# The last twelve expert rows in smaller batches, and the first mixer tile requested at another point, in a two-block float32 kernel

## What is computed

```
def one_block(args):
    xb, ib, gb = args
    ue = jnp.take(u, ib, axis=0)
    a = jnp.einsum('thkd,td->thk', ue, xb, preferred_element_type=jnp.float32)
    w = jax.nn.gelu(a) * gb
    ve = jnp.take(v, ib, axis=0)
    return jnp.einsum('thk,thkd->td', w.astype(ve.dtype), ve)
```

## Time and profile before

| what | value |
|---|---|
| runs | 1396.99, 1397.28, 1399.54 us (median 1397.28) |
| the profiled execution | 1396.25 us, its span 1394.4 us |
| mean granted TensorE clock | 0.962 of full speed |
| PE busy | 1263.6 us |
| DVE busy | 726.9 us |
| gathers | 256, from 297.0 to 954.6 us (issue times) |
| DMA rate while gathers run | about 420 GB/s |

### The profile page before, as it was taken

How to read it: one execution, slowest core, us unless ns; L and a number is a source line. 1 busy time by engine, 2 the same in 40 slices (tenths; PEclk the granted TensorE clock), 3 DMA queues, 4 the chain that set the end, 5 groups by cost and what they waited for, 6 DMA issues and landing times.

```text
span 1394.4 us, 12560 instructions
## 1 busy us (share of the span) xinstructions
PE 1263.6 (91%) x4528; PEld 723.0 (52%) x4528; DVE 726.9 (52%) x1760; ACT 239.9 (17%) x614; POOL 321.8 (23%) x273
## 2 busy tenths in 40 slices
PE   7999999989989888778889897878999999999998
PEld 6757555465545444333334332333456458888743
DVE  3664623178767777777786875654244532100001
ACT  2132221111211111111221112111201431000000
POOL 0100000024434444353545545452000010000000
PEclk9999999999999999898999999999999999999999
DMA  8435577269999999999999999997335363543530
GB/s 292 173 130 181 181 253 275 86 266 422 388 418 421 421 418 420 415 421 407 414 422 421 421 407 421 421 420 320 136 128 181 129 249 133 182 168 111 191 150 31
DMA packets 98669, 398.97 MB, mean 286 GB/s; under 512 B 6384, under 2 KB 9840, under 8 KB 65712
## 3 DMA queue, kind: packets, MB, share of 16 engines
q0 software_dynamic: 37376, 270.29, 46.8%
q1 hardware_dynamic: 61232, 127.88, 25.7%
HBM read 397.09 MB, written 1.05 MB: 286 GB/s over the span
## 4 chain that ended last, share of the span: by engine, by line
PE 61%; DMA 21%; DVE 13%; issue 2%; ACT 2%; POOL 1%; SPq 0%; DVEq 0%; PEldq 0%; ACTq 0%
DMA big<-in_peer_uv,idx_t 21%; PE ps L500 15%; PE ps L512 14%; PE ps L750 10%; DVE big L1795 6%; PE ps L1024 5%; PE ps L719 2%; PE ps L689 2%; PE ps L988 2%; PE ps L972 2%; PE ps L526 1%; POOL big L1396 1%; PE ps L592 1%; ACT rows L1211 1%; PE ps L489 1%
## 5 line engine op out<-in xcount | busy, mean ns | idle before, releaser
L750 PE MATMUL ps<-big,rows 128*128 128x512 f32 x1024 | 491.2, 636 | 103.2 <-ACT rows L1211 103.2
L1396 POOL DMA_INDIRECT big<-in_peer_uv,idx_t x256 | 309.1, 1207 | 391.6 <-PE ps L750 328.8
L750 PEld LDWEIGHTS ps<-big,rows 128*128 128x128 f32 x1024 | 203.2, 203 | 373.2 <-issue 373.2
L1795 DVE CUSTOM_DVE_ANT_0 big<-big 128x1024 f32<-128x1024 f32 x256 | 307.7, 1224 | 144.9 <-DMA big<-in_peer_uv,idx_t 142.1
L500 PE MATMUL ps<-wring,big 128*128 128x512 f32 (+1 forms) x496 | 211.6, 582 | 0.0
L512 PE MATMUL ps<-big,wring 128*128 128x256 f32 x896 | 195.6, 381 | 1.0 <-DVE big L1450 1.0
L512 PEld LDWEIGHTS ps<-big,wring 128*128 128x128 f32 x896 | 171.2, 191 | 25.2 <-issue 1.8
L500 PEld LDWEIGHTS ps<-wring,big 128*128 128x128 f32 x496 | 93.4, 191 | 107.7 <-issue 106.5
L1205 ACT ACTIVATE small<-small 128x4 f32<-128x4 f32 x64 | 13.2, 207 | 513.5 <-DVE small L1800 513.5
L1211 ACT ACTIVATE rows<-const,small 128x128 f32<-128x128 f32 x256 | 81.9, 391 | 19.2 <-DVE small L1804 18.0
L1024 PE MATMUL ps<-wring,big 128*128 128x512 f32 x176 | 75.7, 592 | 0.0
(11 more groups left out here) (243 smaller groups left out, 944.0 us busy)
## 6 DMA issues: line engine op xcount, KB each, us to landing
wring<-in_w_in SPq DMA_DIRECT2D x17, 2048.0 KB, 8.2
wring<-in_w_ada SPq DMA_DIRECT2D x12, 2048.0 KB, 8.6
wring<-in_w_gate SPq DMA_DIRECT2D x5, 2048.0 KB, 7.7
wring<-in_w_up SPq DMA_DIRECT2D x5, 2048.0 KB, 7.9
wring<-in_w_down SPq DMA_DIRECT2D x5, 2048.0 KB, 8.4
wring<-in_w_out SPq DMA_DIRECT2D x4, 2048.0 KB, 13.7
wring<-in_peer_wq SPq DMA_DIRECT2D x4, 2048.0 KB, 7.8
big<-in_peer_uv,idx_t POOLq DMA_INDIRECT x256
```

The source lines that it names most:

```text
L750: last = nc.tensor.matmul(banks[h], diag[:, k % DIAGS, :], v_part[:, ring_at(k), h * 512:(h + 1) * 512], start=False, stop=(k % SLOTS == S ...
L1396: pool.indirect_dma_start(pair_ring[:, ring_at(k), :], None, a["peer_uv"], bass.IndirectOffsetOnAxis(idx_t[:, k:k + 1], 0))\
L1795: nc.vector.tensor_tensor_reduce(u_part[:, ring_at(k), :], u_part[:, ring_at(k), :], h_t[:, b, :], 1.0, 0.0, ALU.mult, ALU.add, a_dot[:, i ...
```

## The change

Batches 0 to 60 keep four rows. The last twelve rows, 244 to 255, were three batches of four; they become five batches of two (244 to 253) and two of one (254, and 255). The number of batches goes from 64 to 68. The small operations, the tanh and the loops work on as many columns as the batch has. The wait of SP before the tile `in2_q` is no longer on `pair_free` (row 249 used by PE) but on `pair_landed` of row 253: the gather of the third last row has landed.

```
-BATCHES = NB * SLOTS // BATCH
 HALF_BATCHES = SLOTS // BATCH
+SIZES = [BATCH] * (NB * HALF_BATCHES - 3) + [2] * 5 + [1, 1]
+BATCHES = len(SIZES)
+FIRST = [sum(SIZES[:m]) for m in range(BATCHES)]
+LAST_ROW = NB * SLOTS - 1
...
                 if name == "in2_q":
-                    sp.wait_ge(pair_free, (BATCHES - 1) * BATCH - 2)
+                    sp.wait_ge(pair_landed[ring_at(LAST_ROW - 2)], 16 * ((LAST_ROW - 2) // RING + 1))
...
-                for k in range(m * BATCH, (m + 1) * BATCH):
+                for k in range(FIRST[m], FIRST[m] + SIZES[m]):
                     pe.wait_ge(pair_landed[ring_at(k)], 16 * (k // RING + 1))
                     pe.wait_ge(diag_built, k + 1)
...
                 act.wait_ge(gelu_in, m + 1)
-                nc.scalar.activation(ge[1], ge[0], ACT.Tanh, scale=GELU_C).then_inc(gelu_exp, 1)
+                n = SIZES[m]
+                nc.scalar.activation(ge[1][:, 0:n], ge[0][:, 0:n], ACT.Tanh, scale=GELU_C).then_inc(gelu_exp, 1)
                 act.wait_ge(w_ready, m + 1)
-                for k in range(m * BATCH, (m + 1) * BATCH):
+                for k in range(FIRST[m], FIRST[m] + SIZES[m]):
                     if k >= DIAGS:
                         act.wait_ge(pair_free, k - DIAGS + 1)
-                    at_w = k % (2 * BATCH)
+                    at_w = m % 2 * BATCH + k - FIRST[m]
...
-                b = m // HALF_BATCHES
-                for i in range(BATCH):
-                    k = m * BATCH + i
+                b, first, n = min(m // HALF_BATCHES, NB - 1), FIRST[m], SIZES[m]
+                dot = a_dot[:, 0:n]
+                g = [t[:, 0:n] for t in ge]
+                for i in range(n):
+                    k = first + i
...
-                dve.wait_ge(dotted, (m + 1) * BATCH)
-                link(tt(ge[2], a_dot, a_dot, ALU.mult))
-                link(ts(ge[2], ge[2], 0.044715, 1.0, ALU.mult, ALU.add))
-                tt(ge[0], ge[2], a_dot, ALU.mult).then_inc(gelu_in, 1)
-                link(stt(ge[3], a_dot, 0.5, gate_t[:, m * BATCH:(m + 1) * BATCH], ALU.mult, ALU.mult))
+                dve.wait_ge(dotted, first + n)
+                link(tt(g[2], dot, dot, ALU.mult))
+                link(ts(g[2], g[2], 0.044715, 1.0, ALU.mult, ALU.add))
+                tt(g[0], g[2], dot, ALU.mult).then_inc(gelu_in, 1)
+                link(stt(g[3], dot, 0.5, gate_t[:, first:first + n], ALU.mult, ALU.mult))
                 dve.wait_ge(gelu_exp, m + 1)
                 at_w = m % 2 * BATCH
-                stt(w_now[:, at_w:at_w + BATCH], ge[1], 1.0, ge[3], ALU.add, ALU.mult).then_inc(w_ready, 1)
+                stt(w_now[:, at_w:at_w + n], g[1], 1.0, g[3], ALU.add, ALU.mult).then_inc(w_ready, 1)
```

## The result

| | before | changed |
|---|---|---|
| median of 6 runs | 1396.69 us | 1390.31 us |
| lowest and highest | 1396.28, 1399.54 | 1388.63, 1390.68 |
| the profiled execution | 1396.25 us | 1390.32 us |
| its span | 1394.4 us | 1388.5 us |

The ratio is 0.995 with a 95% interval of 0.9939 to 0.9961, 5.4 to 8.5 us of gain. In the profiled pair the gain is 5.93 us.

What follows compares the result with a forecast made beforehand. PE bounds most of the kernel, gathers the expert rows; 5.34 us less PE work minus 1.0 us sharing gives 4.3 us, from 1397.28 to 1393.0 us; range 1390.8 to 1396.9.

Steps and rivals of the forecast that it cites:

- ACT's table load: After the last diagonal: ends about 1 us sooner and stays hidden behind the one-row batch.
- that term: Gathers of rows 254 and 255 asked for about 1 us earlier; costed at nothing because requests stand in a full queue.
- The tile is late next: Before the mixer: the tile comes 0.4 us ahead of its use, the next thing to be late.
- 5.34: End of the experts: work behind the last landing falls from four rows to one, 3 x 1.78 us less.
- the request that hangs on batch 60: Row 250's gather: its request hangs on batch 60, left unchanged, so its 3.40 us gap stays.
- Ten packets make 1.0 us: Lagging engine's last gathers: ten 8 KB packets share with the tile at 0.10 us each, costing 1.0 us.
- goes through to the end of the kernel one to one: After the experts: whatever their end gains or loses reaches the kernel's end undiminished.
- 0.92 us: Gap before row 250: gain if it vanished, the upper bound for earlier gather requests, used in the range's lower end.
- Sharing at no cost: Rival, last gathers: the tile does not slow them; gain between 4.7 and 5.3 us, time 1392.3; chance 0.12.
- Even sharing: Rival, lagging engine: rows 254 and 255 lose 3.3 us to the tile; gain 2.0, time 1395.3; chance 0.13.
- the tile ahead of the last row: Rival, lagging engine: the tile's share precedes row 255's packets, delaying landing 6.5 us; time 1398.5; chance 0.07.
- The clock: Rival, new tail: TensorE's clock halves, row 255 costs 1.78 us more; gain 2.5, time 1394.8; chance 0.08.

Runs made afterwards that it cites:

- the run with the old condition: Changed kernel's batch sizes, with SP's old wait (PE has used row 249) in place of row 253's landing; median 1391.48 us, ratio 0.997.
- the first padded run: Kernel before, with 28 tiny memsets added on DVE in the expert rows; median 1396.01 us, ratio 1.0002.
- the request at 960.36: Changed kernel with PSUM banks of the first two mixer products exchanged and the tile requested when row 252 has landed; median 1389.05 us, ratio 0.9953.
- the run at row 248: Changed kernel with the tile requested when row 248 has landed, instead of row 253; median 1394.19 us, ratio 0.998.
- the run at row 254: Changed kernel with the tile requested when row 254 has landed, instead of row 253; median 1389.83 us, ratio 0.995.
- the last split alone: Changed kernel with all batches of four but the last, split into rows 252 to 254 and row 255; median 1394.16 us, ratio 0.9983.
- the tile at row 255: Changed kernel with the tile requested only when the last row has landed; median 1392.75 us, ratio 0.9973.
- the wait alone: Kernel before, old batches of four, with SP's new wait (row 253 has landed); median 1395.94 us, ratio 1.0.

## Why the prediction was wrong in size

*What held.* The last landings set the end of the stage. A row costs PE 1.78 us, and three rows went from behind the last landing. Batches of one fit DVE. ACT's table load stayed hidden (971.06 to 972.34, the copy at 973.38). PE's idle before the mixer is 1.47 us with ACT's copy as its releaser, as I had written. The gather of row 255 was asked for at 950.95, 3.7 us sooner than before and not 1, and row 255 was no sooner there: that term was rightly nothing. The tile is late next: asked for at row 255 it is the bound, at row 254 it is not. The handover's gain is 5.34 - 0.23 (row 255's sum at 968.29, not 968.06) - 0.18 (a row alone takes 1.96 us of PE and not 1.78, by the run with the old condition) = 4.93, which is what the trace shows. About 0.1 us of it is row 253 being there at 963.02 and not at 963.14, which differs from one execution to the next.

*Right for another reason.* The gap before row 250 stayed (952.12, 955.56), as forecast. I had put it down to the request that hangs on batch 60. In the first padded run it stands four rows earlier, together with an instruction fetch, and row 250 has none.

*The step that was mis-sized: "Ten packets make 1.0 us".* The price per packet was right, 0.08 to 0.10. The number was not. Though the tile was requested at 963.07, the last landing was stretched by 0.34 us only, four packets' worth and not ten. The trace shows where: the lagging engine's last 8 KB packets start at about 965.3, 965.6, 965.9, 966.2 and 966.5, still 0.3 us apart, and then at 966.9 and 967.3, 0.4 us apart, as in the run with the old condition. So the first seven of the ten went as if there were no tile, and that engine took its first piece of the tile only at about 966.8, 3.7 us after the request, although the idle engines had tile packets from 964.3 on. With the request at 960.36 row 255 was 0.75 us later than in the changed kernel, at 958.70 1.25, at 950.52 3.7, each counted from an earlier row's sum. The delay grows with how long before the last landing the tile is asked for, but starts late: the gather packets that an engine already has go first. In the run at row 248 that is seen on all engines, with no tile packet for 3.5 us.

The Trainium skill has a rule ("DMA: Bandwidth & Descriptors", "Queues, rings and completion order") by which an engine drains about 9 to 17 descriptors of one queue before it turns to the next. This case's traces do not agree with it: in the run at row 248 one gather packet and one tile packet alternate. Nor does the 0.34 us, since by an estimate from that page and 0.08 us for a piece, even one turn of nine would cost 0.7 us.

*The step that failed: "goes through to the end of the kernel one to one".* The lead at the mixer came through to the last addition with 4.74 of 4.93 us. But the kernel does not end there. The store behind it took 3.2 us before and takes 2.0 now, and no row of mine looked there; I had put what stands behind the last addition at nothing, without a reason. This is 1.2 of the 6 us. The range, whose lower end was made of 5.34 and 0.92 us, had no term for it.

*The base.* I took off from 1397.28, the median of three runs. The median of six is 1396.69, and the kernel before had medians of 1395.8 to 1396.3 beside the experiments. So 0.6 us of the 2.7 us between 1393.0 and 1390.31 is the base, 0.6 us the handover's gain (4.93, not 4.3), and 1.2 us the store, less 0.2 us that the lead lost between the mixer and the last addition. The remaining 0.5 us has no row; executions of one kernel differ by more. Without the store the median would have been 1391.5, inside the range; without the error of the base, or with the right number of packets, it would have been at its edge, by 0.1 us inside.

*The rivals.* Sharing at no cost was the nearest, with 1392.3. Even sharing and the tile ahead of the last row are excluded by the run at row 248. The clock did fall to half in the tail, for 3.4 us, but on rows 250 and 251, with no effect on PE's end. PE had idled for 2.25 us before it, at a place where I had not looked for a pause. In the run with the old condition it idled there for 2.27 us, and the eight records behind took 3.67 us at a granted clock of 1.00. In the run at row 254 the clock stayed full there too, after 2.02 us of idling.

## What to carry to other kernels

Where a stage is bound by arrivals, cut its last batches so that one unit of work is left behind the last arrival, and taper the ones before it, or the engine is still busy with them: here the last split alone gave a third. Ask for the next stage's transfer so that it lands just before its use; here earlier only slowed the arrivals that PE waited for, and later made the tile the bound, with a fall of the clock on top. Leave some room for the packets that are already under way. Before crediting a change with a microsecond, look behind the last instruction: here the final store was 1.2 us longer or shorter by where an instruction fetch fell.

## What the runs showed of the hardware that I had not expected

- One DMA engine lags behind the other fifteen by about 4 us at the end of the gathers (11 packets in 3.3 us at 25 GB/s), so transfers on the others are nearly free then (0.34 us for the whole tile, asked for 5.2 us before the last sum).
- A tile asked for while gathers fill all 16 engines had its first packet 3.5 us after the request (row 248's run), and from then on one packet of 2 KB went with each gather packet (456 and 445 in 10 us).
- A second 8 KB instruction fetch beside a 256 KB store went with a landing of 3.2 us against 2.0: in the two profiles that have it 3.2 us, in the twelve that do not 2.0. 28 added instructions moved it. A fetch also stands in the 0.9 us gap of the gathers at 952 to 956 us, and the gap moved with it.
- The length of a pause alone does not tell whether the clock falls. After 3.49 us (the tile at row 255), 2.25 us (changed) and 2.85 us (the wait alone) PE's records ran partly at half clock; after 3.29 us (row 248's run), 3.16 us (the wait alone, last batch) and 2.27 us (the old condition) they ran at full clock. Before the mixer, pauses of 1.47 us never halved it.
